# Hybrid recurrent trunk on one core: the last layer's residual is turned to rows beside the output tiles, and the final norm's factor is applied to rows

## The reference

```python
def rms_norm(x, gain=None, eps=EPS):
    xf = _f32(x)
    y = xf * lax.rsqrt(jnp.mean(xf * xf, axis=-1, keepdims=True) + eps)
    return y if gain is None else y * gain
...
    # in each layer: four mixer branches, lifted to D_MODEL and merged with sigmoid gates
    merged = jnp.sum(jax.nn.sigmoid(gl) * up, axis=2)
...
```

## Time and profile before

| | |
|---|---|
| time, median of 3 | 1511.96 us |
| time of the profiled execution | 1518.89 us |
| its span in the trace | 1517.1 us |
| mean granted TensorE clock | 0.97 |
| TensorE busy | 1422.2 us, 94% |
| VectorE, ScalarE, GpSimd busy | 659.0, 517.4, 477.3 us |
| HBM read, written | 135.25 MB, 24.89 MB |

### The profile page before, as it was taken

The page is one execution under the profiler, slowest core; times in us unless marked ns, Lnnn a source line. Parts: engine busy times, 40 slices in busy tenths (PEclk is TensorE's granted clock), DMA queues, the critical chain, the costliest instruction groups (busy, mean ns, idle before and its releaser), DMA issues.

```text
span 1517.1 us, 33563 instructions
## 1 busy us (share of the span) xinstructions
PE 1422.2 (94%) x14880; PEld 1288.3 (85%) x14880; DVE 659.0 (43%) x1151; ACT 517.4 (34%) x780; POOL 477.3 (31%) x350
## 2 busy tenths in 40 slices
PE   6799999999999999999979999999999999999896
PEld 4698999988889988776879898999888998888695
DVE  5756414217334334736133851231454242655622
ACT  5533422224522244144443352222542122523322
POOL 0244512224212222147833452222332222311730
PEclk9899999999999999999989999999998999999998
DMA  9532221214331262477743323112263125345821
GB/s 317 187 98 75 70 79 51 63 47 104 102 87 44 68 124 72 137 210 218 234 128 84 95 70 84 44 44 71 66 147 82 45 58 94 102 122 154 251 88 57
DMA packets 275908, 162.18 MB, mean 107 GB/s; under 512 B 86102, under 2 KB 244922, under 8 KB 275252
## 3 DMA queue, kind: packets, MB, share of 16 engines
q1 hardware_dynamic: 274100, 159.06, 38.3%
q10 hardware_dynamic: 1664, 0.98, 0.3%
HBM read 135.25 MB, written 24.89 MB: 106 GB/s over the span
## 4 chain that ended last, share of the span: by engine, by line
PE 77%; DVE 11%; ACT 5%; issue 3%; DMA 3%; SPq 0%; ACTq 0%; POOL 0%; DVEq 0%
PE psA L838 32%; PE psA L846 16%; PE psA L888 5%; PE psB L774 3%; PE psB L784 3%; PE psB L783 3%; PE psB L719 2%; DVE RA L1948 1%; PE psB L961 1%; DVE small_rows L1839 1%; PE psB L971 1%; PE psB L1402 1%; ACT w_hi L1439 1%; DVE small_rows L1840 1%; PE psB L766 1%
## 5 line engine op out<-in xcount | busy, mean ns | idle before, releaser
L710 POOL TENSOR_TENSOR w_lo<-ring,w_hi 128x512 fp32r<-128x512 f32 x274 | 383.2, 1421 | 923.5 <-ACT w_hi L1439 865.4
L838 PE MATMUL psA<-h_hi,w_hi 128*128 128x260 f32 x1984 | 434.7, 302 | 23.2 <-DVE h_lo L1854 13.0
L838 PE MATMUL psA<-h_lo,w_hi 128*128 128x260 f32 x1984 | 410.2, 289 | 0.0
L838 PEld LDWEIGHTS psA<-h_hi,w_hi 128*128 128x128 f32 x1984 | 316.6, 195 | 41.2 <-issue 19.7
L838 PEld LDWEIGHTS psA<-h_lo,w_hi 128*128 128x128 f32 x1984 | 317.1, 195 | 0.2
L846 PE MATMUL psA<-h_hi,w_lo 128*128 128x260 f32 x1984 | 274.5, 286 | 0.0
L846 PEld LDWEIGHTS psA<-h_hi,w_lo 128*128 128x128 f32 x1984 | 249.6, 187 | 5.3 <-issue 1.0
L1439 ACT CAST w_hi<-ring 128x1024 fp32r<-128x1024 f32 x133 | 137.2, 1033 | 13.9 <-PE psA L846 4.2
L789 ACT COPY ws<-psB 128x128 f32<-128x128 f32 x80 | 21.5, 269 | 244.2 <-PE psB L774 244.2
L797 DVE COPY_PREDICATED tg<-tmask,psB 128x128 f32<-128x128 uint8 x40 | 14.2, 356 | 127.9 <-PE psB L784 78.1
L1469 ACT ACTIVATE tg<-psA 128x520 f32<-128x520 f32 x48 | 28.9, 602 | 96.8 <-PE psA L846 96.5
(11 more groups left out here) (476 smaller groups left out, 2336.4 us busy)
## 6 DMA issues: line engine op xcount, KB each, us to landing
ring<-in_w_in SPq DMA_DIRECT2D x122, 512.0 KB, 4.2
scr_tanh<-tg SPq DMA_DIRECT2D x48, 260.0 KB, 4.6
ring<-in_ada_w SPq DMA_DIRECT2D x18, 512.0 KB, 4.8
upw<-in_w_up SPq DMA_DIRECT2D x64, 128.0 KB, 3.5
RA<-scr_tanh SPq DMA_DIRECT2D x30, 260.0 KB, 3.5
RB<-in_ada_w SPq DMA_DIRECT2D x14, 512.0 KB, 4.9
ws<-scr_tanh SPq DMA_DIRECT2D x24, 260.0 KB, 4.1
ring<-in_w_out SPq DMA_DIRECT2D x9, 512.0 KB, 5.3
```

Source lines behind the costliest of these rows:

```text
L710: nc.gpsimd.tensor_tensor(tile_part(RL[s][:, k], (kind, n)), tile_part(RS[s][:, k], (kind, n)), tile_part(HS[L.hslot[q]][:, k], (kind, n)) ...
L838: nc.tensor.matmul(out(h), HS[L.hslot[q]][:, p, 0:m], cols(part(p), h), start=(p == 0 and part is hi), stop=False)
```

## The change

It touches the last part of layer 1 alone, and the block behind it.

In the loop over the output tiles, VectorE multiplies each finished tile of x by `final_g` into `hT` (step `xg`). TensorE transposes that tile of `hT` one iteration later (`turn`: four pieces of 128 positions into one bank of `psB`, and the 8 samples into another), in the place where the sums of squares stood. ScalarE copies the turned pieces to `ws` (`turn_out`). The squares that ScalarE makes are added up over the 8 tiles by VectorE (`sum_squares`, step `acc`), and TensorE sums the result over the channels once, by 5 float32 matmuls with one column of ones, so that the sums stand with positions on the partitions. ScalarE makes the factor from them: `rs_col`, one column for each 128 positions and one for the samples. In the last block the rows in `ws` are multiplied by their factor, rows 0 and 2 (groups of 128 positions) and the samples by VectorE, 1 and 3 by ScalarE, and sent from two queues, SP's and ScalarE's. Layer 0 stays as it is.

```diff
--- before.py
+++ after.py
...
         mid = sb("mid", [P, 2, NC])
+        rs_col = sb("rs_col", [P, 5])
...
+            sq_last = [ws[:, 10 + d % 2, :] for d in range(KT)]
+            sq_sum = ws[:, 12, :]
+            turned = ws[:, 0:8, :].rearrange("p (t a) c -> p t a c", a=2)
...
+                def turn(d):
+
+                    pe.wait_ge(*dve_f.at("xg", d))
+                    if d >= 2:
+                        pe.wait_ge(*act_f.at("turned", d - 2))
+                    for t in range(4):
+                        nc.tensor.transpose(psB[:, d % 2, t * P:(t + 1) * P], hT[:, d, t * P:(t + 1) * P], ident)
+                    nc.tensor.transpose(psB[0:NB, 3 - d % 2, 0:P], hT[:, d, SEQ:TT], ident).then_inc(*pe_f.step("turn"))
+
...
+                    if layer:
+                        if e:
+                            turn(e - 1)
+                        continue
                     if e == 2:
                         square_sums(0)
                     if e >= 2:
                         square_sums(e - 1)
-                square_sums(KT - 1).then_inc(*pe_f.step("ss"))
+                if layer == 0:
+                    square_sums(KT - 1).then_inc(*pe_f.step("ss"))
+                else:
+                    turn(KT - 1)
+                    pe.wait_ge(*act_f.at("turned", KT - 2))
+                    pe.wait_ge(*dve_f.at("acc", KT - 2))
+                    for t in range(4):
+                        nc.tensor.matmul(psB[:, 0, t:t + 1], sq_sum[:, t * P:(t + 1) * P], ones[:, 0:1], start=True, stop=True)
+                    nc.tensor.matmul(psB[0:NB, 0, 4:5], sq_sum[:, SEQ:TT], ones[:, 0:1], start=True, stop=True).then_inc(*pe_f.step("ss"))
 
...
+
+                def turn_out(d):
+
+                    act.wait_ge(*pe_f.at("turn", d))
+                    cols = slice((d % 4) * P, (d % 4 + 1) * P)
+                    nc.scalar.copy(turned[:, :, d // 4, cols], psB[:, d % 2, :].rearrange("p (t c) -> p t c", t=4))
+                    nc.scalar.copy(ws[0:NB, 8 + d // 4, cols], psB[0:NB, 3 - d % 2, 0:P]).then_inc(*act_f.step("turned"))
...
                 for e in range(KT):
                     split_ahead("out", e)
                     for n in L.out_pieces[e]:
                         mod_rows(n)
                     act.wait_ge(*dm.at("x", e))
+                    if layer:
+                        if e >= 2:
+                            act.wait_ge(*dve_f.at("acc", max(0, e - 3)))
+                        A(sq_last[e], xT[:, e, :], ACT.Square).then_inc(*act_f.step("sq"))
+                        if e:
+                            turn_out(e - 1)
+                        continue
                     A(ws[:, 2 + e, :], xT[:, e, :], ACT.Square).then_inc(*act_f.step("sq"))
                     if layer == 0 and e >= KT - 2:
                         act.wait_ge(*tile_done(*LAYERS[1].hprev[e - KT + 2]))
                         first_split(act, e - KT + 2, LAYERS[1])
+                if layer:
+                    turn_out(KT - 1)
+                    act.wait_ge(*pe_f.at("ss"))
+                    A(rs_col[:, 0:4], psB[:, 0, 0:4], ACT.Ln, bias=eps, scale=1.0 / D_MODEL)
+                    A(rs_col[0:NB, 4:5], psB[0:NB, 0, 4:5], ACT.Ln, bias=cc("eps", 0, NB), scale=1.0 / D_MODEL).then_inc(*act_f.step("lnx"))
+                    act.wait_ge(*act_f.at("lnx"))
+                    A(rs_col[:, 0:4], rs_col[:, 0:4], ACT.Exp, scale=-0.5)
+                    A(rs_col[0:NB, 4:5], rs_col[0:NB, 4:5], ACT.Exp, scale=-0.5).then_inc(*act_f.step("rs"))
+                    act.wait_ge(*act_f.at("rs"))
+                    return
...
+                def sum_squares(k):
+
+                    dve.wait_ge(*act_f.at("sq", k + 1))
+                    did(dve_f, "acc", T_(sq_sum, sq_sum if k else sq_last[0], sq_last[k + 1], add), k)
+
...
                     did(dm, "x", T_(xT[:, e, SEQ:TT], xT[:, e, SEQ:TT], der[:, 32:40], add), e)
-        pe9, act9, dve9 = track("pe9"), track("act9"), track("dve9")
+                    if layer:
+                        S_(hT[:, e, :], xT[:, e, :], par("final_g", e), None, mult).then_inc(*dve_f.step("xg"))
+                        if e >= 2:
+                            sum_squares(e - 2)
+                if layer:
+                    sum_squares(KT - 2)
+
+
+
+
+        act9, dve9 = track("act9"), track("dve9")
+        y_rows = lambda t: ws[:, 2 * t:2 * t + 2, 0:512]
+        y_out = lambda t: o["y_prompt"][0, t * P:(t + 1) * P, :].rearrange("p (a c) -> p a c", a=2)
 
         @block.scalar
         def _(act):
-            for t in range(4):
-                act.wait_ge(*pe9.at("y", t))
-                ps = psA if t % 2 == 0 else psB
-                nc.scalar.copy(ws[:, 2 * t:2 * t + 2, 0:512], ps[:, 0:2, :]).then_inc(*act9.step("y"))
-
-        @block.tensor
-        def _(pe):
-            pe.wait_ge(*dve9.at("y"))
-            for t in range(4):
-                ps = psA if t % 2 == 0 else psB
-                if t >= 2:
-                    pe.wait_ge(*act9.at("y", t - 2))
-                for d in range(KT):
-                    last = nc.tensor.transpose(ps[:, d // 4, (d % 4) * P:(d % 4 + 1) * P], hT[:, d, t * P:(t + 1) * P], ident)
-                last.then_inc(*pe9.step("y"))
-            for d in range(KT):
-                last = nc.tensor.transpose(psA[0:8, 2 + d // 4, (d % 4) * P:(d % 4 + 1) * P], hT[:, d, SEQ:TT], ident)
-            last.then_inc(*pe9.step("ys"))
+            for n, t in enumerate((1, 3)):
+                nc.scalar.activation(y_rows(t), y_rows(t), mybir.ActivationFunctionType.Identity, scale=rs_col[:, t:t + 1]).then_inc(*act9.step("y"))
+                act.wait_ge(*act9.at("y", n))
+                act.dma_start(y_out(t), y_rows(t)).then_inc(s_y, 16)
 
         @block.vector
         def _(dve):
             dve.wait_ge(*TR["act_f"].at("rs"))
-            for d in range(KT):
-                last = nc.vector.scalar_tensor_tensor(hT[:, d, :], xT[:, d, :], par("final_g", d), rs[:], mult, mult)
-            last.then_inc(*dve9.step("y"))
-            dve.wait_ge(*pe9.at("ys"))
-            nc.vector.tensor_copy(ws[0:8, 8:10, 0:512], psA[0:8, 2:4, :]).then_inc(*dve9.step("ys"))
+            dve.wait_ge(*TR["act_f"].at("turned", KT - 1))
+            for t in (0, 2):
+                nc.vector.tensor_scalar(y_rows(t), y_rows(t), rs_col[:, t:t + 1], None, mult).then_inc(*dve9.step("y"))
+            nc.vector.tensor_scalar(ws[0:NB, 8:10, 0:512], ws[0:NB, 8:10, 0:512], rs_col[0:NB, 4:5], None, mult).then_inc(*dve9.step("y"))
 
         @block.sync
         def _(sp):
-            for t in range(4):
-                sp.wait_ge(*act9.at("y", t))
-                sp.dma_start(o["y_prompt"][0, t * P:(t + 1) * P, :].rearrange("p (a c) -> p a c", a=2), ws[:, 2 * t:2 * t + 2, 0:512]).then_inc(s_y, 16)
-            sp.wait_ge(*dve9.at("ys"))
-            sp.dma_start(o["y_sample"][:, 0, :].rearrange("p (a c) -> p a c", a=2), ws[0:8, 8:10, 0:512]).then_inc(s_y, 16)
+            for n, t in enumerate((0, 2)):
+                sp.wait_ge(*dve9.at("y", n))
+                sp.dma_start(y_out(t), y_rows(t)).then_inc(s_y, 16)
+            sp.wait_ge(*dve9.at("y", 2))
+            sp.dma_start(o["y_sample"][:, 0, :].rearrange("p (a c) -> p a c", a=2), ws[0:NB, 8:10, 0:512]).then_inc(s_y, 16)
             sp.wait_ge(s_y, 16 * 5)
     return {n: t.made for n, t in tracks.items()}
 
```

More of the change, by code:

```diff
@@ L2427 @@
     'dve_m0': 'mul mul mul mul mul mul mul mul mul mg mul mg mul mg mul mg mul mg mul mg mul mg mul mg mul mg mul mg mul mg mul mg mul mg mul mg mul mg mul mg mul mg mul mg mlo mul mg mlo mul mg mlo mul mg mlo mul mg mlo mul mg mlo mul mg mlo mlo xs x xs x xs x xs x xs x xs x xs x xs x'.split(),
-    'pe_f1': 'st ada ada ada ada ada ada mod ada ada mod ss'.split(),
-    'act_f1': 'hh hhd hh hh hh hh hh hh hh lam_abs lam_z expA modrow modrow sq sq sq sq sq sq sq sq lnx rs'.split(),
-    'dve_f1': 'hg hr hs hd hs hld hl hs hl hs hl hs hl hs hl hs hl hs hl hl zero der lam1 lam2 lam3 lam4 lam5 lamm13 lama13 lamm11 lama11 lamm9 lama9 lamm7 lama7 lamm5 lama5 lamm3 lama3 lamm1 lama1 lam6 lam_y lam_sp stT modT gate'.split(),
+    'pe_f1': 'st ada ada ada ada ada ada mod ada ada mod turn turn turn turn turn turn turn turn ss'.split(),
+    'act_f1': 'hh hhd hh hh hh hh hh hh hh lam_abs lam_z expA modrow modrow sq sq turned sq turned sq turned sq turned sq turned sq turned sq turned turned lnx rs'.split(),
+    'dve_f1': 'hg hr hs hd hs hld hl hs hl hs hl hs hl hs hl hs hl hs hl hl zero der lam1 lam2 lam3 lam4 lam5 lamm13 lama13 lamm11 lama11 lamm9 lama9 lamm7 lama7 lamm5 lama5 lamm3 lama3 lamm1 lama1 lam6 lam_y lam_sp stT modT gate xg xg xg acc xg acc xg acc xg acc xg acc xg acc acc'.split(),
     'pe_a1': 'crow lora lora kks bsum gram gram tr tr z gram y z y z gram y z y z tr y tr z z gram y x1 z u y o z gram y x1 z u y o z tr y tr z z gram y x1 z u y o z gram y x1 z u y o z tr y tr z z y x1 z u y o z y x1 z u y o z y z x1 u o x1 u o mt'.split(),
@@ L2455 @@
```

(5 more changed lines are left out.)

## The result

| | before | changed |
|---|---|---|
| median (runs) | 1513.18 us (11) | 1508.16 us (11) |
| lowest, highest | 1503.96, 1526.24 us | 1501.28, 1514.20 us |
| profiled execution, its span | 1518.89, 1517.1 us | 1503.75, 1501.9 us |

The ratio is 0.9944, with a 95% interval of 0.9917 to 0.9970: faster by 8.5 us of 1513, between 4.5 and 12.6. In a second measurement it was 0.9951 (0.9921 to 0.9981; medians 1507.24 us of 12 runs, against 1514.20 of 23 for the kernel before). Both kernels spread over more than 10 us, so I take the ratio, which puts 1503.5 us against the 1511.96 from which the prediction started.

A forecast was written before the change was run, and what follows sets the result against it. TensorE was taken to bound most of the program, then a chain of engines working alone and the output transfer's rate. Loop 1.0 + chain 6.6 = 7.6 us off the 1511.96 us median gave 1504.4 us, range 1501.5 to 1507.5.

The forecast's parts named there:

- the chain: Behind the last product: work ahead of the first output issue shrinks, so that issue comes 6.6 us earlier.
- The loop: Output tiles ahead of the last product's end: sums removed (4.7 us), six turns added (3.7), so 1.0 us shorter.
- What a turn waits for: In the loop: inputs are ready well before each turn; VectorE's and ScalarE's added work is covered by a 5.7 us product.
- case 3: Rival, in the loop: turns start 1.1 us late, waiting for VectorE or ScalarE; six cost 6.6 us, time 1511; chance 0.05.
- P: Moment when the last product's last weight load is followed by tile 6's sums of squares, 1494.22 in the kernel before.
- case 5: Rival, behind the last product: ScalarE's back-to-back copies overlap, saving up to 0.6 us; 1503.8 us; chance 0.04.
- None is late: Output transfer: every later group is ready in time, so first issue to end stays at 8.13 us.
- case 4: Rival, at the end: slower two-queue transfer, late one-column sums, half-pace multiplication; 2.0 us less gain, 1506.4 us; chance 0.12.
- Case 2: Rival, in the loop: transposes count as rest, TensorE's clock falls; 21 to 35 us more, 1525 to 1539; chance 0.04.
- The carrying over to a median: Last step of the sum: the saving on the profiled execution, 6.9 us above the median, is applied to the median.

## Why the prediction was right

**The direction and the mechanism.** The forecast was 7.6 us off the time, by a shorter chain behind the last product and a shorter loop, with the transfer unchanged behind its first issue. The ratio gives 8.5 us, the cuts 8.7, and each part came out the way forecast. Faster by over 0.2% had 0.91. The two large terms erred to the same side, the loop by 0.9 and the chain by 0.4 us, so the sum was not helped by errors that cancel.

**The loop, forecast 1.0 us, measured 1.9.** This is the term that was off most, by both of its parts. The sums of squares were sized by the distance of their first weight load to the next product's first, 0.77 us; they cost 5.2/6 = 0.86. The next product's first loads ran slower behind them, as the earlier trace rows show already: two loads at 1481.72 take 0.41 us, where two in the changed kernel behind a turn take 0.30:

```profile
1480.11 0.30 PEld L843 LDWEIGHTS psA<-merged_hi,w_hi 128*128 128x128 f32 x2
```

Five such places, with 0.11 us each, are the 0.5 us that were missing. The turns were taken at 0.116 us for each transpose and 0.03 us on top; the last of the five loads only 8 columns (0.09 us), and a turn takes 0.54 to 0.55.

**What a turn waits for.** Nothing in the loop, as argued, so case 3 fell: TensorE was busy for all of the 38.00 us shown above. VectorE's added work was longer than its rows while GpSimd split weights: its product by `final_g` took 1.57 us for tile 1, with GpSimd's two instructions from 1449.55 on, and 0.49 us for the tiles after GpSimd had finished.

```profile
1449.55 2.73 POOL L715 TENSOR_TENSOR w_lo<-ring,ra_lo 128x512 fp32r<-128x512 f32 x2 [4.40 <-ACT ra_lo L1465]
...
1449.56 1.57 DVE L2405 TENSOR_SCALAR hT<-xT,parT 128x520 f32<-128x520 f32 x1
...
1457.34 1.78 DVE L2386 TENSOR_TENSOR ws<-ws 128x520 f32<-128x520 f32 x1
...
1474.82 0.49 DVE L2405 TENSOR_SCALAR hT<-xT,parT 128x520 f32<-128x520 f32 x1
```

It was hidden, since a product covers 5.8 us (34.59 / 6; the prediction has 5.7 from three times 1.9, though the start in the earlier trace rows gives 1.80 for the last third, and so 5.4; nothing hung on it).

**Behind P.** With P at 1485.87 in the changed kernel: the table load starts at P + 3.65 (forecast 3.93), Exp ends at P + 6.95 (7.3), the first issue is at P + 7.77 (8.15). The four copies put the table load off by 1.43 us and not by 1.71, as they overlap, which is what case 5 said; a group of 128 x 1024 takes VectorE about 0.75 us. The sums ended at P + 4.69, ahead of the table as forecast, by 0.24 us in this run; in the first run with one queue they were late by 0.60, by the clock.

**The transfer.** 8.26 us against 8.13. "None is late" holds. Two queues gain nothing, as argued from the earlier trace rows; they cost 0.2. Of the terms of case 4 none came but this.

**The clock.** Case 2 fell: the clock stayed at 1.00 in the loop with the turns as they are and with four times as many. Where a low clock does enter is not in the loop but behind it, and by 0.6 us (the first run with one queue). The Trainium skill, "TensorE: Matmul & The Clock Gate", Part 4, says that the full clock doesn't come on for transposes; the trace disagrees. In the last block of the kernel before it rose from 0.50 to 1.00 while only transposes ran (at 1509 in the earlier trace rows, at about 1521.5 in its second profile), and in the fourfold turns it stayed at 1.00 over forty transposes in a row, from 1498.6 to 1503.0.

**The carrying over to a median** was the weakest step. How far the profiled execution lies from the median depends on how long the clock was low ahead of the loop, which goes from 54 to 99 us in the twelve profiles and moved the part ahead by 20 us. The range allowed a little over a microsecond either way for this; that the ratio fell within 1 us of the forecast is in part luck, as its interval is 8 us wide.

## What to carry to other kernels

A normalizing factor can be applied after the last layout change when it is one number a row, so that the layout change need not wait for it. Here this moved 30 of 40 transposes ahead of the last product's end, and left one group of rows to be multiplied ahead of the first output instead of eight tiles, at a price of 1.4 us of copies. But look at each part by itself: the turns' place beside the tiles was worth 1.55 us, and the largest share, by the run with the turns behind the loop, came from letting another engine add up the squares (5.2 us in the loop). When a chain that crosses engines is shortened, look for what stands between the last two: the table load behind ScalarE's copies was worth 0.7 us, and a single useless instruction earlier removed it. When runs spread by more than the change, cut the profiles at instructions that both kernels share: the loop repeated within 0.03 us, while the spans of one kernel differed by 10.

## What was not expected of the hardware

- A product's first two weight loads behind the sums of squares (float32 matmuls of 260 columns) take longer: 0.41 us, against 0.30 behind transposes.
- A float32 matmul of one column stands in the profile as two instructions of 0.111 us each at full clock, no less than a transpose of 128 columns, which is one; with the clock low for most of them, eight took 1.84 us instead of 1.02.
- VectorE's 128x520 multiplication, 0.49 us alone, took 1.5 to 1.6 us while GpSimd worked, and an addition 1.8 instead of 0.7 us; GpSimd's two instructions took 2.7 us in place of 2.5. Which of the two gives way in what order was not tested.
- Where the clock falls behind the last product varies by more than a microsecond from run to run: from the stretches' means it fell 2.7 us behind the cut at tile 7 in the first run with one queue (at 1492.1), and 5.0 us behind it in the profile of the changed kernel, by a mean of 0.82 from 1491 to 1492 (at 1491.6):

```profile
1491.00:1492.00 1.00, 0.00 (x0) 0.82 0.00 0
```
